# The first five units of a hybrid decoder layer: products from x times gain, the norm applied on the way out of PSUM

## What is computed

```python
def _rmsnorm(x, g):
    y = x * rsqrt(mean(x * x, axis=-1, keepdims=True) + EPS) * g
    return y
h = _rmsnorm(x, g_pre_mix)
proj = h @ w_in                     # 1024 -> 7680 columns
qa, fa, ia, ga, qb, kb, vb, uc, gl = split(proj)
```

## Time and profile before

| | us |
|---|---|
| median of 3 runs | 2318.68 |
| lowest and highest run | 2316.85, 2319.75 |
| profiled execution: span, first to last instruction (the page lists no other time of it) | 2321.0 |
| PE busy | 2147.9 (93%) |
| DVE busy | 1079.1 (46%) |
| ACT busy | 604.1 (26%) |
| POOL busy | 589.4 (25%) |
| first product of unit 0 starts at | 29.56 |
| last product of the prefix ends at | 99.54 |

### The profile page before, as it was taken

The page is one execution under the profiler, slowest core; times in us unless marked ns, Lnnn a source line. Parts: engine busy times, 40 slices in busy tenths (PEclk is TensorE's granted clock), DMA queues, the critical chain, the costliest instruction groups (busy, mean ns, idle before and its releaser), DMA issues.

```text
span 2321.0 us, 31837 instructions
## 1 busy us (share of the span) xinstructions
PE 2147.9 (93%) x12704; PEld 2005.6 (86%) x12704; DVE 1079.1 (46%) x1169; ACT 604.1 (26%) x760; POOL 589.4 (25%) x392
## 2 busy tenths in 40 slices
PE   6999999999999999999978889789999999999994
PEld 5887898878988899878968889579999999999993
DVE  4277555775367663765534652452222223222235
ACT  3234412343223432345123421220100101001011
POOL 1221112211111211211112232343232333323322
PEclk9997999989998999989989999899999999999997
DMA  4220204102131121312144333201111120111132
GB/s 141 57 93 28 58 28 127 52 19 67 47 114 37 48 56 58 101 39 58 38 159 149 111 102 120 102 14 55 32 50 41 41 59 29 52 45 36 54 106 79
DMA packets 203987, 156.89 MB, mean 68 GB/s; under 512 B 15730, under 2 KB 188402, under 8 KB 203890
## 3 DMA queue, kind: packets, MB, share of 16 engines
q1 hardware_dynamic: 201698, 146.89, 20.4%
q10 hardware_dynamic: 2192, 8.65, 1.0%
HBM read 120.16 MB, written 35.35 MB: 67 GB/s over the span
## 4 chain that ended last, share of the span: by engine, by line
PE 85%; DVE 7%; ACT 5%; issue 1%; DMA 1%; POOL 0%; POOLq 0%; SPq 0%; DVEq 0%; ACTq 0%
PE psum L364 69%; PE psum L601 4%; PE psum L621 3%; PE psum L666 3%; PE psum L612 2%; PE psum L569 1%; DVE hid L1482 1%; PE psum L648 1%; DVE mix L1467 1%; PE psum L630 1%; DVE arena L1170 1%; DVE x_again L1461 0%; DMA conv_full<-c_d 0%; DVE hid_lo L1484 0%; DVE mix L1457 0%
## 5 line engine op out<-in xcount | busy, mean ns | idle before, releaser
L364 PE MATMUL psum<-h_hi,w_hi 128*128 128x352 f32 x2400 | 541.7, 334 | 37.1 <-DVE h_lo L1174 10.9
L364 PE MATMUL psum<-h_hi,w_lo 128*128 128x352 f32 x2400 | 525.7, 327 | 0.0
L364 PE MATMUL psum<-h_lo,w_hi 128*128 128x352 f32 x2400 | 525.6, 328 | 0.0
L364 PEld LDWEIGHTS psum<-h_hi,w_hi 128*128 128x128 f32 x2400 | 412.1, 193 | 75.9 <-issue 53.1
L364 PEld LDWEIGHTS psum<-h_hi,w_lo 128*128 128x128 f32 x2400 | 419.8, 191 | 0.0
L364 PEld LDWEIGHTS psum<-h_lo,w_hi 128*128 128x128 f32 x2400 | 416.3, 192 | 0.0
L341 POOL CAST w_hi<-w_raw 128x1024 fp32r<-128x1024 f32 x60 | 71.9, 1198 | 913.7 <-PE psum L364 895.1
L354 POOL CAST w_hi<-w_raw 128x512 fp32r<-128x512 f32 (+1 forms) x128 | 96.5, 754 | 732.5 <-PE psum L364 643.3
L356 POOL TENSOR_TENSOR w_lo<-w_raw,w_hi 128x512 fp32r<-128x512 f32 (+1 forms) x128 | 229.7, 1794 | 10.3
L1140 ACT ACTIVATE hid<-psum 128x1056 f32<-128x1056 f32 x32 | 33.7, 1054 | 583.1 <-PE psum L364 583.1
L364 PE MATMUL psum<-hid_hi,w_hi 128*128 128x352 f32 x768 | 166.4, 325 | 10.8 <-DVE hid_lo L1484 10.8
(11 more groups left out here) (226 smaller groups left out, 2459.8 us busy)
## 6 DMA issues: line engine op xcount, KB each, us to landing
w_raw<-in_w_in SPq DMA_DIRECT2D x60, 512.0 KB, 4.0
w_raw<-in_w_ff SPq DMA_DIRECT2D x32, 512.0 KB, 4.0
w_raw<-in_w_ff SPq DMA_DIRECT2D x64, 256.0 KB, 2.7
g_d<-gate_logits SPq DMA_DIRECT2D x24, 528.0 KB, 2.7
gates<-g_d SPq DMA_DIRECT2D x24, 528.0 KB, 3.6
arena<-in_xT SPq DMA_DIRECT2D x8, 528.0 KB, 7.0
x_again<-in_xT SPq DMA_DIRECT2D x1, 4224.0 KB, 13.8
x_d<-x_again ACTq DMA_DIRECT2D x8, 528.0 KB, 2.7
```

What stands on the lines that cost most here:

```text
L364: mm = pe.matmul(ps[:, b0 + g, 0:GW], w[:, slot, k, :], x[:, k, g * GW:(g + 1) * GW], start=(k == 0 and w is wh and x is xh), stop=(k == k ...
```

## The change

x is no longer normalised ahead of the prefix. ACT multiplies each chunk by the gain alone and rounds it (xg_hi), DVE makes the low part from x, the gain and xg_hi (xg_lo); PE multiplies these for the five units of the prefix. The norm is a factor of each token, so it commutes with the product, and DVE multiplies each unit by `rs1` when it takes it out of PSUM. The sum of squares goes another way: ACT squares, DVE adds the eight squared chunks up, PE sums the one result over channels in three products that stand within unit 1. Units use banks 0 to 2 and 3 to 5 in turn. The normalised h_hi and h_lo, which the later units need, are still made, by the same operations, while PE works on the prefix. The weights of unit 0 are loaded ahead of x, those of unit 1 right behind it. x now lies where h_lo will be, and the prefix's own tiles lie over tiles that only the groups use.

Cut to its core:

```diff
         @block.sync
+            sp.dma_start(pk[:, 0:KD], dr["params"][:, 0:KD]).then_inc(gains_in, 16)
+            load_unit2(sp, 0, 0, B_COLS[0])
             for f in range(KD):
                 sp.dma_start(xT[:, f, :], dr["xT"][f * P:(f + 1) * P, :]).then_inc(x_in[f], 16)
-            sp.dma_start(pk[:, :], dr["params"]).then_inc(const_in, 16)
+            load_unit2(sp, 1, 0, B_COLS[1])
+            sp.dma_start(pk[:, KD:], dr["params"][:, KD:]).then_inc(const_in, 16)
...
-            sp.wait_ge(h_ready, KD)
+            sp.wait_ge(unit_done, PRE)
...
         @block.tensor
+            def prefix_part(u, ks):
+                if 0 in ks:
+                    pe.wait_ge(w_split, u + 1)
+                    if u >= 2:
+                        pe.wait_ge(staged.sem, u - 1)
+                for k in ks:
+                    if u == 0:
+                        pe.wait_ge(xg_ready, k + 1)
+                    mm = product(pe, u % 2, (k,), KD, xh, xl, 3 * (u % 2))
+                if KD - 1 in ks:
+                    mm.then_inc(unit_done, 1)
+            def square_sums(gs_):
+                for g in gs_:
+                    if g == 2:
+                        pe.wait_ge(x_logs, 1)
+                    pe.matmul(ps[:, 6 + g % 2, 0:GW], ones[:, :], xsq7[:, g * GW:(g + 1) * GW],
+                              start=True, stop=True).then_inc(x_sums, 1)
...
+            prefix_part(0, range(KD))
+            prefix_part(1, range(0, 4))
+            pe.wait_ge(x_added, KD - 1)
+            square_sums((0, 1))
+            prefix_part(1, range(4, 6))
+            square_sums((2,))
+            prefix_part(1, range(6, KD))
+            for u in range(2, PRE):
+                prefix_part(u, range(KD))
+            pe.wait_ge(staged.sem, PRE - 1)
+            pe.wait_ge(h_ready, KD)
...
         @block.scalar
             for f in range(KD):
                 act.wait_ge(x_in[f], 16)
+                act.activation(xh[:, f, :], xT[:, f, :], IDN, scale=par("g_pre_mix", f)).then_inc(xg_hi_set, 1)
                 if f >= 2:
-                    act.wait_ge(x_summed, f - 1)
-                act.activation(sq1[:, f % 2, :], xT[:, f, :], ACT.Square).then_inc(x_squared, 1)
+                    act.activation(x_square(f - 2), xT[:, f - 2, :], ACT.Square).then_inc(x_squared, 1)
...
-            for u in range(PRE):
-                stage(u, 0, *B_DST[u])
...
         @block.vector
+            def x_low(f):
+                dve.wait_ge(xg_hi_set, f + 1)
+                dve.scalar_tensor_tensor(xl[:, f, :], xT[:, f, :], par("g_pre_mix", f), xh[:, f, :].bitcast(F32),
+                                         ALU.mult, ALU.subtract).then_inc(xg_ready, 1)
+            def stage(u):
+                dve.wait_ge(unit_done, u + 1)
+                src, dst = psg(3 * (u % 2)), v3((kT, vT, qT, ua, ug)[u][:, :])
+                if u == 2:
+                    ins = dve.scalar_tensor_tensor(dst, src, DH ** -0.5, v3(rs1), ALU.mult, ALU.mult)
+                else:
+                    ins = dve.tensor_tensor(dst, src, v3(rs1), ALU.mult)
+                ins.then_inc(staged.sem, 1)
...
+            for f in range(KD):
+                x_low(f)
+                if f >= 4:
+                    x_add(f - 3)
+            for f in range(5, KD):
+                x_add(f)
+            dve.wait_ge(h_rstd, 1)
+            stage(0)
             dve.wait_ge(const_in, 32)
             dve.tensor_copy(levm[:, :, :].rearrange("p l t -> p (l t)"), mask_f[:, 0:NL * P])
             dve.tensor_copy(keep[:, :], mask_f[:, NL * P:])
+            for f in range(4):
+                h_of(f)
+            stage(1)
+            for f in range(4, KD):
+                h_of(f)
+            for f in range(3):
+                h_low(f)
+            stage(2)
+            for f in range(3, KD):
+                h_low(f)
+            stage(3)
+            stage(4)
```

More of the change, by code:

```diff
@@ L112, in build @@
         s_h.close()
+        s_x = ExitStack()
+        sb("h_hi_room", [P, KD, T], F32, s_x)
+        xT = sb("x_first", [P, KD, T], F32, s_x)
+        s_x.close()
         bf = sb("ob_full", [P, NH, T], F32)
@@ L145, in build @@
         s2.close()
+        s1 = ExitStack()
+        xsq = sb("x_squares", [P, KD - 1, T], F32, s1)
+        mask_f = sb("masks_in", [P, NL * P + T], F32, s1)
+        sb("mask_rest", [P, 2 * T - NL * P - T], F32, s1)
+        xh = sb("xg_hi", [P, KD, T], F32R, s1)
+        xl = sb("xg_lo", [P, KD, T], F32R, s1)
+        rs1 = sb("x_rstd", [P, T], F32, s1)[:, :]
+        xsq7 = sb("x_square_last", [P, T], F32, s1)[:, :]
+        s1.close()
         s3 = ExitStack()
@@ L191, in build, with x_square @@
         neg = par("neg", 0, P)
[L193 to L196, removed]
+        def x_square(f):
+            return xsq[:, f, :] if f < KD - 1 else xsq7
         S = lambda name, per=0, before=0: Signal(sem(name), per, before)
@@ L203, in build @@
         ones_set = sem("ones_set")
-        x_squared = sem("x_squared")
-        x_summed = sem("x_summed")
+        gains_in = sem("gains_in")
+        xg_hi_set, xg_ready = sem("xg_hi_set"), sem("xg_split")
+        x_squared, x_added = sem("x_squared"), sem("x_squares_added")
+        x_sums, x_logs = sem("x_square_sums"), sem("x_square_logs")
         h_rstd = sem("h_rstd")
@@ L370, in _ @@
         def _(sp):
+            sp.dma_start(pk[:, 0:KD], dr["params"][:, 0:KD]).then_inc(gains_in, 16)
+            load_unit2(sp, 0, 0, B_COLS[0])
             for f in range(KD):
                 sp.dma_start(xT[:, f, :], dr["xT"][f * P:(f + 1) * P, :]).then_inc(x_in[f], 16)
[L373 to L374 removed]
+            load_unit2(sp, 1, 0, B_COLS[1])
+            sp.dma_start(pk[:, KD:], dr["params"][:, KD:]).then_inc(const_in, 16)
+            sp.dma_start(mask_f[:, :], dr["masks"]).then_inc(const_in, 16)
             sp.dma_start(pages[:, :], dr["pages"]).then_inc(pages_in, 16)
[L376 removed]
+            for u in range(2, PRE):
                 load_unit2(sp, u, 0, B_COLS[u])
@@ L864, in _ @@
             lnexp()
+            psg = lambda b0: ps[:, b0:b0 + G, 0:GW]
+            v3 = lambda ap: ap.rearrange("p (g t) -> p g t", g=G)
+            act.wait_ge(gains_in, 16)
+            act.wait_ge(ones_set, 2)
             for f in range(KD):
                 act.wait_ge(x_in[f], 16)
+                act.activation(xh[:, f, :], xT[:, f, :], IDN, scale=par("g_pre_mix", f)).then_inc(xg_hi_set, 1)
                 if f >= 2:
-                    act.wait_ge(x_summed, f - 1)
-                act.activation(sq1[:, f % 2, :], xT[:, f, :], ACT.Square).then_inc(x_squared, 1)
[L870 to L875, removed]
+                    act.activation(x_square(f - 2), xT[:, f - 2, :], ACT.Square).then_inc(x_squared, 1)
+            for f in (KD - 2, KD - 1):
+                act.activation(x_square(f), xT[:, f, :], ACT.Square).then_inc(x_squared, 1)
+            for g in range(G):
+                act.wait_ge(x_sums, g + 1)
+                act.activation(rs1[:, g * GW:(g + 1) * GW], ps[:, 6 + g % 2, 0:GW], ACT.Ln, bias=eps[:, 0:1],
+                               scale=1.0 / D).then_inc(x_logs, 1)
+            act.wait_ge(x_logs, G)
             act.activation(rs1, rs1, ACT.Exp, scale=-0.5).then_inc(h_rstd, 1)
@@ L1164, in _, with x_add, h_of, h_low @@
             dve.memset(cwp[:, 0:1], 0.0).then_inc(oa_stored.sem, 1)
+            def x_low(f):
+                dve.wait_ge(xg_hi_set, f + 1)
+                dve.scalar_tensor_tensor(xl[:, f, :], xT[:, f, :], par("g_pre_mix", f), xh[:, f, :].bitcast(F32),
+                                         ALU.mult, ALU.subtract).then_inc(xg_ready, 1)
+            def x_add(f):
+                dve.wait_ge(x_squared, f + 1)
+                if f > 1:
+                    dve.wait_ge(x_added, f - 1)
+                dve.tensor_tensor(xsq7 if f == KD - 1 else xsq[:, 0, :], xsq[:, 0, :], x_square(f), ALU.add)\
+                    .then_inc(x_added, 1)
+            def stage(u):
[6 more added lines that the diff above has]
+                ins.then_inc(staged.sem, 1)
+            def h_of(f):
+                dve.scalar_tensor_tensor(xT[:, f, :], xT[:, f, :], par("g_pre_mix", f), rs1, ALU.mult, ALU.mult)\
+                    .then_inc(h_full, 1)
+            def h_low(f):
+                dve.wait_ge(h_hi_set, f + 1)
+                dve.tensor_tensor(hl[:, f, :], xT[:, f, :], hh[:, f, :].bitcast(F32), ALU.subtract)\
+                    .then_inc(h_ready, 1)
+            dve.wait_ge(gains_in, 16)
+            for f in range(KD):
[6 more added lines that the diff above has]
+            stage(0)
             dve.wait_ge(const_in, 32)
```

2 lines of the change are left out of this document (1 added, 1 removed).

## The result

The changed kernel took **2292.59 us** in the median (2291.45 to 2294.51, 4 runs), the kernel before beside it 2317.76 (2314.82 to 2319.75, 4 runs): a ratio of 0.9882 [0.9863, 0.9902]. The profiled execution took 2293.09, its span is 2291.3. Forecast were 2297.2, and 2291.5 to 2302.5. The gain is 25.2 us by the medians, 27.4 by the ratio, where 21.5 were expected.

The account below looks back on a forecast made before the run. PE, busy 93% of the span, bounds the kernel, so time is won only where it waits. The prefix ending at 78 instead of 99.54 gains 21.5 us: 2318.7 - 21.5 = 2297.2, range 2291.5 to 2302.5.

Parts of the forecast that it names:

- E: Moment when the prefix's last product ends in the new kernel: forecast 78, against 99.54 in the old, 21.5 us gained.
- rival A: POOL's two splits fall between DVE's operations in the prefix: E = 73.7, 26 us gained, 2292.8; chance 0.15.
- the wait of 0.2 near 66: Before unit 4, PE stalls 0.1 to 0.7 us, taken as 0.2, for DVE's copy of unit 2.
- Unit 0 at full speed: Prefix's first unit: products priced at the 2.4 GHz level; at 1.2 GHz E would be 4.4 us later.
- rival B: Unit 0 at the lower clock, or DVE slower where sets change: 17 us gained, 2301.6; chance 0.16.
- My row at 35 to 40 us: Old kernel's prefix: PE busy 3.63 of 5.00 us, spaced by DVE, clock 1.00; used to price unit 0.
- The rule of the Trainium skill: A kernel pausing at each tile repeatedly drops to the lower clock; by it the gain would be 17, not 21.5.
- Nothing late in the first group: Behind the prefix, copies and SP's weight loads delay nothing: last copy costs 0 or 0.1 us, loads 0.
- The cover of 0.2: First group's last weights: landing 3.9 us before POOL's split, against at most 3.7 us of delay; taken as 0.
- Behind it PE goes on as before, so E minus 99.54 is the change.: After the prefix PE's time stays the same, if nothing in the first group comes late; the change is 21.5 us.
- C: First group waits elsewhere, above all for SP's loads, so nothing is gained: within 0.2%; chance 0.04.
- D: Lower clock for the whole prefix, PE's five units: 46.8 us cost against 21.5 gained, 2344; chance 0.03.

Follow-up runs that it names:

- e9: Changed kernel, only that POOL waits for the last addition of squares before it splits unit 2's weights: 2308.08 us (one execution).
- e16: The changed kernel unchanged, run again for comparison: 2289.63 us, ratio 0.9877 to the kernel before.
- e11: e10 with 30 unread products of ones by ones on PE ahead of the prefix: 2291.34 us, ratio 0.9879 to the kernel before.
- e10: Changed kernel with low parts and xg_hi ahead of squares and additions, first two sums a chunk later, unit 2's split after the additions: 2295.22 us, ratio 0.9879.

## Why the prediction was right or wrong

**The prefix: right, to 0.2 us in three of four profiles.** Last low part of x 26.5 (25.9 forecast), sum of squares whole 34.4 (34.0), unit 2 at 42.6 (42.1), E 77.85 (78.0). Both of POOL's splits met DVE, as the earlier trace rows had it, so rival A did not come; e9 shows the price. That the sum hit so well is partly luck, since small misses cancelled. Late were x's first chunk, used at 7.2, not 6.4, and unit 2, by 0.5. Early was DVE, which paid 3.0 and 2.6 for the two splits, not 3.4 each. Three units that follow one another directly took 35.27, not 35.7, and the wait of 0.2 near 66 is absent: q's copy ended at 65.17, and PE wanted its banks at 66.1.

**"Unit 0 at full speed": wrong for its first chunks, hidden in three profiles, and in e16 rival B.** In the first profile, in 10.70 to 16.10 us 18 products took 5.40, 0.30 each, the length that goes with a clock of 0.50 in e16's window. It cost nothing, because DVE set the pace (e11 took it away and gained nothing). I had priced B at 4.4 for the whole of unit 0; in e16 it struck the last chunk of unit 0 and the first of unit 1, and cost 2.3. My row at 35 to 40 us was of a PE that had worked since 5.8; here it starts from rest. The rule of the Trainium skill, "TensorE: Matmul & The Clock Gate", section "HAM oscillation — how this bites in real kernels", that I set aside, bears on one of the four profiles of this kernel: in e16 the clock fell behind a pause, once. In the other three it did not.

**Nothing late in the first group: right.** SP's group loads began at 82.03, E + 4.2, and the split of the unit that I had watched waited for its DMA:

```profile
82.03 0.70 SPq L413 DMA_DIRECT2D arena<-in_conv_prev  x1
...
106.25 1.04 POOL L355 CAST w_hi<-w_raw 128x1024 fp32r<-128x1024 f32 x1 [10.86 <-DMA w_raw<-in_w_in]
```

That is E + 28.4; in the earlier trace rows it was E + 28.05. The cover of 0.2 that I had figured is used up, and PE does not wait for it.

**The step that failed: "Behind it PE goes on as before, so E minus 99.54 is the change."** The order of work is as before, the pace is not. Over all executions the gain is 26.4 ± 3.1: the prefix gives about 21 (21.5 to 21.7 in three profiles, 19.4 in e16), the rest 5.4 ± 3.1 through its granted clock, and 8.0 in the first pair of profiles. The term was mis-sized at 0, and so was the range: I gave it 1 us on either side, after three runs of before that lay within 3 us, while 22 executions of the changed kernel reach from 2282.6 to 2311.3. On the forecast's own base of 2318.7 the measured ratio gives 2291.3, below the range's 2291.5; the median of 2292.59 lies just inside it. The page's line of granted clock below 9 in several slices, and the windows of the groups at 0.92 to 0.95, were there to be read (0.92 in 920.4 to 1089.9 us of the kernel before). They would have widened the range; why the clock is higher behind the new prefix, no run here shows.

**Rivals.** A's time, 2292.8, is almost the median, by luck: its mechanism was absent, both splits fell on DVE. C and D did not come: units 2 to 4 took 35.27 us for 216 products.

## What to carry to other kernels

A second PSUM set and a late scale are worth far more together than one by one, because the set lets PE go on while the scale is being found. An operation of POOL that meets a DVE busy with operations on two SBUF tiles cost DVE most of its own length (2.6 to 3.0 of 3.4 us here) wherever it was put in the queue, so move it to where DVE is idle, not to another place in the queue. When a clock below full speed is granted over most of a kernel, a few us won at the start are measured against a spread of over 20 between executions, and a prediction's range has to hold that spread.

## What the runs showed of the hardware

- The mean granted clock of the same 12297 products differed from kernel to kernel: 0.9537 ± 0.0006 behind the old prefix, 0.9573 ± 0.0014 behind the new one, and 0.9545 ± 0.0021 in two variants of the new one (e10 and e11). Each 0.001 is 1.8 us here. What sets it stays open.
- The clock's column reads 1.00 in 10.70 to 16.10 us of the changed kernel, while the products have the length of the lower level. In the first microseconds the products' lengths tell more than the column.
- The same program kept a clock of 1.00 behind waits of PE of 1.84 to 1.98 us (three profiles) and fell to 0.50 behind one of 2.39, with 0.54 more a chunk later (e16).
